# Layer 0's weight stream in the order of use, a key rotation on GpSimd, and folded squares

## The reference, cut to what matters

```python
def mla_mixer(h, cos, sin, w_a, g_q, w_uq, g_kv, w_ukv, w_o):
    a = h @ w_a                                   # 1024 -> 384 + 256 + 64
    cq, ckv, kr = jnp.split(a, [Q_LORA, Q_LORA + KV_LORA], axis=-1)
    q = (rms_norm(cq, g_q) @ w_uq).reshape(B, S, MLA_HEADS, NOPE_DIM + ROPE_DIM)
    q_nope = q[..., :NOPE_DIM]
    q_rope = apply_rope(q[..., NOPE_DIM:], cos[:, :, None], sin[:, :, None])
    kv = (rms_norm(ckv, g_kv) @ w_ukv).reshape(B, S, MLA_HEADS, NOPE_DIM + V_DIM)
    k_nope, v = kv[..., :NOPE_DIM], kv[..., NOPE_DIM:]
    k_rope = apply_rope(kr, cos, sin)
    ...                                           # masked softmax attention, o
    return o @ w_o

h = rms_norm(x, attn_pre_g[layer])                # x0; x1, x2, x3 are the next norms
```

## Time and profile before

| | us |
|---|---|
| median of 3 runs | 991.06 |
| lowest, highest | 990.77, 992.12 |
| the profiled execution | 990.73 |
| its span, first to last instruction | 988.6 |

### The profile page before, as it was taken

One profiled execution on the slowest core, in us unless ns is written; L12 is line 12 of the kernel. 1 busy time (PEld: TensorE's weight loads), 2 busy tenths in 40 slices (PEclk: granted clock), 3 DMA queues, 4 the chain that ended last, 5 costly groups with the idle time before them and its releaser, 6 DMA issues.

```text
span 988.6 us, 18855 instructions
## 1 busy us (share of the span) xinstructions
PE 959.7 (97%) x7951; PEld 923.9 (93%) x7951; DVE 721.8 (73%) x1342; ACT 542.7 (55%) x837; POOL 17.3 (2%) x48
## 2 busy tenths in 40 slices
PE   6999999999999999999999999999999999999997
PEld 6978999999998988799999998898999999999996
DVE  5965788887657877699878888646654879888653
ACT  6635565454436556565545444546755567676542
POOL 0000000000000000000000000000130000000000
PEclk9999999999999999999999999999999999999999
DMA  7433467676664742438666883543333545555521
GB/s 288 182 128 128 193 221 280 225 252 259 263 212 154 269 147 109 171 146 323 247 265 256 328 317 122 214 175 125 129 131 130 209 171 186 199 185 199 212 89 43
DMA packets 28452, 194.71 MB, mean 197 GB/s; under 512 B 3280, under 2 KB 3536, under 8 KB 5456
## 3 DMA queue, kind: packets, MB, share of 16 engines
q1 hardware_dynamic: 28368, 193.51, 52.7%
HBM read 192.45 MB, written 1.05 MB: 196 GB/s over the span
## 4 chain that ended last, share of the span: by engine, by line
PE 85%; DVE 7%; ACT 5%; issue 2%; DMA 1%; SPq 1%; POOL 0%; DVEq 0%; ACTq 0%
PE bank L495 24%; PE bank L496 23%; PE bank L501 23%; DVE s_wlo L1343 2%; PE bank L625 2%; PE bank L651 2%; ACT s_whi L883 2%; PE bank L556 2%; PE bank L550 2%; PE bank L551 1%; PE bank L515 1%; PE bank L522 1%; PE bank L516 1%; PE bank L635 1%; DMA s_raw<-in_wa 1%
## 5 line engine op out<-in xcount | busy, mean ns | idle before, releaser
L1343 DVE TENSOR_TENSOR s_wlo<-s_raw,s_whi 128x512 fp32r<-128x512 f32 (+1 forms) x364 | 371.3, 1061 | 141.1 <-ACT s_whi L883 140.7
L883 ACT ACTIVATE s_whi<-s_raw 128x1024 fp32r<-128x1024 f32 (+2 forms) x233 | 305.3, 1336 | 212.2 <-PE bank L501 198.2
L495 PE MATMUL bank<-s_hh,s_whi 128*128 128x256 f32 x1400 | 393.6, 281 | 0.4 <-DVE s_hl L1425 0.2
L496 PE MATMUL bank<-s_hl,s_whi 128*128 128x256 f32 x1400 | 387.6, 277 | 0.0
L501 PE MATMUL bank<-s_hh,s_wlo 128*128 128x256 f32 x1383 | 382.8, 277 | 0.0
L495 PEld LDWEIGHTS bank<-s_hh,s_whi 128*128 128x128 f32 x1400 | 263.3, 188 | 6.2 <-issue 5.1
L496 PEld LDWEIGHTS bank<-s_hl,s_whi 128*128 128x128 f32 x1400 | 263.1, 188 | 0.1
L501 PEld LDWEIGHTS bank<-s_hh,s_wlo 128*128 128x128 f32 x1383 | 259.8, 188 | 0.0
L495 PE MATMUL bank<-s_ph,s_whi 128*128 128x256 f32 x528 | 146.4, 277 | 0.0
L496 PE MATMUL bank<-s_pl,s_whi 128*128 128x256 f32 x528 | 145.8, 276 | 0.0
L501 PE MATMUL bank<-s_ph,s_wlo 128*128 128x256 f32 x516 | 142.5, 276 | 0.0
(11 more groups left out here) (237 smaller groups left out, 1278.9 us busy)
## 6 DMA issues: line engine op xcount, KB each, us to landing
s_raw<-in_gu SPq DMA_DIRECT2D x44, 1024.0 KB, 4.9
s_raw<-in_dn SPq DMA_DIRECT2D x33, 1024.0 KB, 4.8
s_raw<-in_wada SPq DMA_DIRECT2D x24, 1024.0 KB, 5.1
s_raw<-in_up SPq DMA_DIRECT2D x22, 1024.0 KB, 4.8
s_raw<-in_wo SPq DMA_DIRECT2D x8, 1024.0 KB, 4.8
s_raw<-in_win_g SPq DMA_DIRECT2D x8, 1024.0 KB, 4.8
s_raw<-in_wkv_v SPq DMA_DIRECT2D x4, 1024.0 KB, 5.3
s_raw<-in_wkv_k SPq DMA_DIRECT2D x4, 1024.0 KB, 4.8
```

The lines of the kernel that those rows point to most:

```text
L495: e.matmul(out, hi, xh[:, k, :], start=first, stop=False, skip_group_check=True)
L496: e.matmul(out, hi, xl[:, k, :], start=False, stop=False, skip_group_check=True)
L883: e.activation(whi[w % SPLIT][:, at], raw[p % RAW][:, at], ACT.Copy).then_inc(S.hi.tick((w, c0)), 1)
L1343: e.tensor_tensor(wlo[s][:, at], raw[p % RAW][:, at], whi[s][:, at].bitcast(F32), ALU.subtract).then_inc(S.lo.tick((i, j), (i, "all")), 1)
```

## The change

- **Loads.** The nine columns needed first (norm weight and frequencies), the positions and x become one tensor of 16 + 256 + 8 x 256 columns. SP loads it in two transfers, the first with the columns, the positions and two row blocks of x, the second with the other six. The first piece of `wa` comes in two halves, not in four quarters. The other columns (`cols`) are loaded after piece 2.
- **Programs at the start.** ACT and DVE have a new order for the splits of x and `wa`, the angles and the squares. ACT makes sine and cosine ahead of the squares and of its part of piece 1.
- **PE's first work.** PE starts with 16 matmuls of ones by ones, 128 columns, into a bank that nobody reads.
- **Layer 0's stream.** The tiles of `wuk`, `wuq` and `wuv` are laid in one weight stream `mla`, in the order in which PE uses them. Only `wuk` 0 to 3 stand ahead of `_order0()`; the other keys, the values and the queries are mixed with the softmax steps, with new paces and places.
- **Key rotation.** Its six operations move from DVE to POOL, behind POOL's constants.
- **Folds.** x0, x1, x2 and x3 get `fold` on DVE and one matmul of ones instead of two; the columns of x2 are two matmuls instead of four.

```diff
+WARM = 16
+FRONT = 16 + T
+MLA = ([("wuk", i) for i in range(4)] + [("wuq", i) for i in range(12)] +
+       [("wuk", i) for i in range(4, 8)] + [("wuq", i) for i in range(12, 24)] + [("wuv", i) for i in range(16)] +
+       [("wuk", i) for i in range(8, 12)] + [("wuq", i) for i in range(24, 30)] +
+       [("wuk", i) for i in range(12, 16)] + [("wuq", i) for i in range(30, 36)])
+MLA_AT = {unit: i for i, unit in enumerate(MLA)}
+STREAM = [("wa", 56), ("mla", 68), ("wo0", 64), ("gu0", 352), ("dn0", 176),
...
+PACE0 = {"wuk": 0.72, "wuq": 0.84, "wuv": 0.2, "wo0": 0.26}
+PAIR0 = (18, 18, 44, 44)
+AFTER0 = {**AFTER, "exp": ("scores", 9), "scale": ("exp", 3), "values": ("turn1", 7), "chunk": ("values", 0)}
+
+
 def _units(name):
     return [(name, t) for t in range(COUNT[name])]
 
 
 def _order0():
-    units = _units("wuq")[:16] + [("wuv", g) for g in range(8)] + _units("wuq")[16:] + _units("wo0")
-    return _mixed(units, _soft_steps(range(4)), {"wuq": 0.3, "wuv": 0.6, "wo0": 0.3},
-                  lambda p: ("wuq", (17, 29, 35)[p - 1]) if p else ("wuv", 0), "wo0", 2)
+    units = [(name, i // 2 if name == "wuv" else i) for name, i in MLA[4:] if name != "wuv" or i % 2 == 0] + _units("wo0")
+    return _mixed(units, _soft_steps(range(4)), PACE0, lambda p: units[PAIR0[p]], "wo0", 2, AFTER0)
...
-            e.dma_start(cols[:, 0:NFIRST], a["cols"][:, 0:NFIRST]).then_inc(S.gain_in.tick("gain"), 16)
-            e.dma_start(xT[:, 0:2, :], a["xT"][:, 0:2, :]).then_inc(S.x_in[0].tick("x"), 16)
+            first = FRONT + 2 * T
+            e.dma_start(x_front[:, 0:first], a["xT"][:, 0:first]).then_inc(S.x_in[0].tick("x"), 16)
...
                 if i == 0:
-                    for c in range(4):
-                        into = S.first_in[c] if c < 3 else S.raw_in[0]
-                        e.dma_start(dst[:, 512 * c:512 * (c + 1)], src[:, 512 * c:512 * (c + 1)]).then_inc(
-                            into.tick(0), 16)
-                        if c == 0:
-                            e.dma_start(posi, a["pos"]).then_inc(S.pos_in.tick("pos"), 16)
-                        if c in (1, 3):
-                            at = slice(c + 1, c + 3)
-                            e.dma_start(xT[:, at, :], a["xT"][:, at, :]).then_inc(S.x_in[(c + 1) // 2].tick("x"), 16)
-                    e.dma_start(xT[:, 6:8, :], a["xT"][:, 6:8, :]).then_inc(S.x_in[3].tick("x"), 16)
-                    e.dma_start(cols[:, NFIRST:NCOL], a["cols"][:, NFIRST:NCOL]).then_inc(S.cols_in.tick("cols"), 16)
+                    e.dma_start(dst[:, 0:1024], src[:, 0:1024]).then_inc(S.first_in.tick(0), 16)
+                    e.dma_start(x_front[:, first:], a["xT"][:, first:]).then_inc(S.x_in[1].tick("x"), 16)
+                    e.dma_start(dst[:, 1024:2048], src[:, 1024:2048]).then_inc(S.raw_in[0].tick(0), 16)
                 else:
                     e.dma_start(dst[:, 0:k * P], src).then_inc(S.raw_in[i % RAW].tick(i), 16)
+                if i == 2:
+                    e.dma_start(cols[:, NFIRST:NCOL], a["cols"][:, NFIRST:NCOL]).then_inc(S.cols_in.tick("cols"), 16)
...
-                        e.matmul(out[:, T + b:T + b + 1], sq[:, b * P:(b + 1) * P], ones[:, 0:1], start=True, stop=False)
-                        m = e.matmul(out[:, T + b:T + b + 1], sq[:, T + b * P:T + (b + 1) * P], ones[:, 0:1],
-                                     start=False, stop=True)
+                        for half in range(acc):
+                            at = half * T + b * P
+                            m = e.matmul(out[:, T + b:T + b + 1], sq[:, at:at + P], ones[:, 0:1], start=half == 0,
+                                         stop=half == acc - 1)
...
+            q.wait_ge(S.const, "ones")
+            for _ in range(WARM):
+                e.matmul(banks[7][:, 0:P], ones[:, :], ones[:, :], start=True, stop=True, skip_group_check=True)
             q.wait_ge(S.const, "ready")
             lead("wa", 4, 8, hh, hl, "h0", (0, 1), S.dve_out)
-            sums("x0", 7)
+            sums("x0", 7, acc=1)
             tiles("wa", 4, 1, 8, hh, hl, "h0", 2, S.dve_out)
             tiles("wa", 5, 2, 8, hh, hl, "h0", 3, S.dve_out)
             tiles("wuk", 0, 2, 2, cqh, cql, "cq", 4, S.dve_out)
             sums("kv", 6, columns=True)
...
-            tiles("wuk", 2, 2, 2, cqh, cql, "cq", 5, S.dve_out)
-            sums("q", 7)
-            for n in (4, 6):
-                tiles("wuk", n, 2, 2, cqh, cql, "cq", (0, 1)[n // 2 - 2], S.dve_out)
...
+            x_high(0)
+            x_high(1)
+            hi_part(2)
+            hi_part(2)
+            for k in range(2, 6):
+                x_high(k)
+            hi_part(2)
+            hi_part(2)
+            x_high(6)
+            x_high(7)
             q.wait_ge(S.rot, "angle")
             q.wait_ge(S.const, "ready")
             e.activation(sinb, tmp[2][:, :], ACT.Sin).then_inc(S.trig.tick("sin"), 1)
             e.activation(tmp[0][:, :], tmp[2][:, :], ACT.Abs).then_inc(S.trig.tick("abs"), 1)
             q.wait_ge(S.trig, "abs")
             e.activation(cosb, tmp[0][:, :], ACT.Sin, scale=-1.0, bias=epsc[:, 1:2]).then_inc(S.trig.tick("cos"), 1)
+            x0_square(0)
+            hi_part(2)
+            hi_part(2)
+            x0_square(1)
+            x0_square(2)
+            hi_part(3)
+            x0_square(3)
+            hi_part(3)
...
+            angle(0)
+            angle(1)
+            x_low(0)
+            angle(2)
+            x_low(1)
+            lo_part(1)
+            angle(3)
+            lo_part(1)
+            for k in range(2, 6):
+                x_low(k)
+                angle(k + 2)
+            lo_all(1)
+            x_low(6)
+            x_low(7)
+            lo_all(2)
             for i in (1, 2, 3):
                 square_sum("x0", i, sqv[i])
+            fold("x0")
...
-            q.wait_ge(S.dve_out, ("cq", 6))
-            rotate(tmp[3][:, :], tmp[4][:, :], A0.K[:, 8, :], A0.K[:, 9, :], "k")
             lo_all(_used_up("wa", 48) + SPLIT)
-            for n in (0, 2, 4, 6):
-                scaled_out("wuk", n, 2, Rs[1], "kv", lambda m: A0.K[:, m, :])
-                if n == 2:
-                    lo_all(_used_up("wa", 56) + SPLIT)
+            lo_all(_used_up("wa", 56) + SPLIT)
+            scaled_out("wuk", 0, 2, Rs[1], "kv", lambda m: A0.K[:, m, :])
 
...
@@ vector_program, in its walk over _order0()
+                elif step == "wuk":
+                    if i % 4 == 3:
+                        scaled_out("wuk", i // 4 * 2, 2, Rs[1], "kv", lambda m: A0.K[:, m, :])
+                    if i % 2 == 1:
+                        lo_part(_mla_used(step, i) + SPLIT)
...
@@ vector_program, behind the squares of x1; the same line for x2 and x3
+            fold("x1")
...
+            q.wait_ge(S.trig, "cos")
+            q.wait_ge(S.dve_out, ("cq", 6))
+            e.tensor_tensor(tmp[0][:, :], tmp[4][:, :], sinb, ALU.mult)
+            e.tensor_tensor(tmp[1][:, :], tmp[3][:, :], sinb, ALU.mult)
+            e.tensor_tensor(A0.K[:, 8, :], tmp[3][:, :], cosb, ALU.mult)
+            e.tensor_tensor(A0.K[:, 9, :], tmp[4][:, :], cosb, ALU.mult).then_inc(S.rot_k.tick("products"), 1)
+            q.wait_ge(S.rot_k, "products")
+            e.tensor_tensor(A0.K[:, 8, :], A0.K[:, 8, :], tmp[0][:, :], ALU.subtract)
+            e.tensor_tensor(A0.K[:, 9, :], A0.K[:, 9, :], tmp[1][:, :], ALU.add).then_inc(S.rot_k.tick("k"), 1)
```

More of the change, by code:

```diff
@@ L45 @@
           ("up2", 704 // 2), ("dn2", 176)]
-FINE = ("wa", "wuk", "wuv", "wuq", "wo0", "dn0", "wkv_v", "wkv_k", "wq1", "wo1", "dn1", "win_v", "win_k", "win_q", "win_g")
+FINE = ("wa", "mla", "wo0", "dn0", "wkv_v", "wkv_k", "wq1", "wo1", "dn1", "win_v", "win_k", "win_q", "win_g")
 def _stream():
@@ L138, in _stick_steps, with _mixed @@
             yield "keep", p
-def _mixed(units, steps, paces, pair_at, chunk_name, per=1):
+def _mixed(units, steps, paces, pair_at, chunk_name, per=1, after=AFTER):
     steps, ahead, at, made, credit = iter(steps), [], {}, set(), 0.0
@@ L159, in ready @@
         else:
-            need, tiles = (AFTER[name][0], i), AFTER[name][1]
+            need, tiles = (after[name][0], i), after[name][1]
         return need in at and n >= at[need] + tiles
@@ L374, in col @@
             at = COLS[name][0] + j
-            return cols[:, at:at + n]
+            return x_front[:, at:at + n] if at < NFIRST else cols[:, at:at + n]
         def tile_out(name, j):
@@ L684, in tensor_program @@
             for step, i in _order0():
-                if step == "wuq":
+                if step == "wuk":
+                    n, k = i // 2, i % 2
+                    if n % 2 == 0 and k == 0:
+                        bank_of["wuk", n] = (4, 0, 1, 3)[n // 2]
+                        take(bank_of["wuk", n], S.dve_out, ("wuk", n))
+                    q.wait_ge(S.xlo, ("cq", k))
+                    product("wuk", i, banks[bank_of["wuk", n - n % 2]][:, (n % 2) * T:(n % 2 + 1) * T], cqh, cql, k,
```

(33 more changed lines are left out.)

72 lines of the change are left out of this document (38 added, 34 removed).

## The result

| | before | after |
|---|---|---|
| median, us | 991.23 (4 runs) | 983.32 (4 runs: 982.33 to 984.05) |
| profiled execution, its span | 990.73, 988.6 | 982.33, 980.3 |

The ratio is 0.9923, 95% interval 0.9909 to 0.9937: 7.9 us or 0.8% faster. The forecast was 984.6 us, 6.5 us gained, in a range from 981.5 to 988.5. The two profiled executions differ by 8.4 us, and nearly all of that arises in the first 110 us of the program.

What follows compares the result with a forecast made beforehand. PE was taken as the bound, busy in 97% of the span, with DVE full beside it in layer 0. Gains of 2.6, 3.0 and 0.9 us made 6.5 off 990.73, or 984.2; the median forecast was 984.6, range 981.5 to 988.5.

Steps and rivals of the forecast that it cites:

- two signs of being wrong: PE waiting for `s_wlo` between 20 and 43 us, or the first rows of x landing later than 4.7 us.
- Loads and the first product: Start of layer 0: x at 8.2, piece 1 at 12, k = 2 at 12.6; x0's sum ends at 22.3 instead of 24.9.
- The clock behind the wait for k = 2: PE's standstill of some 2 us there may lower its clock, costing 1.7 us; half of it was taken.
- PE at the first scores: PE, with 5.6 us less work ahead of layer 0's first scores, arrives there at 43.4.
- DVE at the first scores: DVE starts `cq` at 23.7 and is ready at 43.7, which sets the first scores: 2.6 us gained.
- POOL's price: Key rotation in layer 0: six POOL operations cost DVE 0.35 us each, 2.1 in all, from possible 0 to 10.5.
- rival in which POOL holds DVE off: Key rotation: operations of 1.2 us, nine tenths lost, cost DVE 6.5 us; ready at 48.1, total 989.0. Chance 0.09.
- Behind the first scores: Layer 0 after the first scores: 3.6 us of PE waits go, less 0.6 for new ones: 3.0 us gained.
- deduction of 0.6 for new waits: Behind the first scores, new short waits because DVE has more keys and a rotation there: 0.6 us lost.
- Folds: Folds outside layer 0's start: x1 gains 0.43, x2 0.43 and 0.40, x3 loses 0.35; 0.9 us gained.
- all in time: No clock fall, POOL free beside DVE: x0's sum at 21.0, PE at 42.1, total 982.3. Chance 0.13.
- the new order is worth only its filled place at the output unit: Waits behind the first scores stay; only the filled place at `wo0` pays, 1.4 instead of 3.0: 986.2. Chance 0.08.

Runs made afterwards that it cites:

- e6: The changed kernel without the sixteen matmuls of ones on PE: 982.37 us, ratio 0.9911.
- e1: The kernel before with the new start alone (loads, new order of ACT and DVE, matmuls of ones, fold of x0): 989.02 us, ratio 0.998.
- e5: The changed kernel with the key's rotation back on DVE: 982.08 us, ratio 0.9906.
- e7: The changed kernel with DVE's four parts of the value weights behind the first evictions and the queries' rotation, and x3 unfolded: 981.28 us, ratio 0.9896.
- e9: The changed kernel once more, unaltered, as the yardstick for e10: 982.66 us, ratio 0.9908.
- e10: The changed kernel with the key's rotation back on DVE, measured beside e9: 981.59 us, ratio 0.99.
- e2: The kernel before with layer 0's new stream and order alone, rotation still on DVE and the old start: 986.08 us, ratio 0.9952.
- e4: The kernel before with the folds of x1, x2 and x3 alone: 990.23 us, ratio 0.999.
- e3: The kernel before with the key's rotation on POOL alone: 989.64 us, ratio 0.9987.
- e11: The kernel of e8 with the key's rotation back on DVE: 979.80 us, ratio 0.9881.
- e12: The kernel of e8 once more, unaltered: 979.63 us, ratio 0.9883.
- e8: e7 plus, at the start, one low part of piece 0 between x's splits and ACT's first high part of piece 1 before the sine: 979.68 us, ratio 0.9882.

## Why the prediction was right

Sign, size and most steps hold; 983.32 lies 1.3 us below the forecast, and neither of its two signs of being wrong came (the first x is used at 4.00, and PE waits for no `s_wlo` between 20 and 43 us). Between the two profiled executions 8.4 us were gained where the sum said 6.5.

- **Loads and the first product: right in place.** x was forecast for 8.2, seen at 8.61; k = 2 for 12.6, seen at 12.86; piece 1 was no longer waited for. A late k = 0 (7.79) cost nothing, and the ones were worth nothing, as costed and as e6 shows. The two lists of SP's issues differ by six, not by five as the prediction has it; no number of its sum hangs on that.
- **The clock behind the wait for k = 2: it falls in some executions.** Half of 1.7 us was put in. In the profiled execution the clock stayed up, so x0's sum ends at 21.7 (21.29 and two rows of 0.22), not at 22.3. In e1, e5 and e7, with a start of the same loads and a wait of 1.9 to 2.0 us, it fell, and the sum stood at 22.94, 22.91 and 22.54; in e9 and e10 it did not. That is three of six, at 1.5 to 1.7 us each. An average was the right thing to put in; no execution shows it.
- **PE at the first scores: forecast 1.3 us too late.** It was to arrive at 43.4 and came at 42.1 (the row at 43.60 less its wait and a part explained below): 0.6 from x0's sum, 0.7 because the stretch took 20.4 us instead of 21.1. The 0.118 us per matmul, which the forecast took as fixed, was not: behind x0's sum 256 columns took 0.116 us on average, from start to start, where before they took 0.120. As DVE was last here, this gained nothing.
- **DVE at the first scores: right, 43.7 against 43.60.** It began at 23.61 (forecast 23.7). POOL's price was put at 2.1 us; it was 1.64 in longer parts and 0.47 in a new wait for ACT, together 2.1. The agreement of the total is partly luck, since the wait for ACT was not foreseen and both numbers vary (e9: 2.13 and 0.67). The rival in which POOL holds DVE off had the right mechanism with too high a price: most operations met DVE for 1.2 us but cost it only about 0.4. The Trainium skill, "SBUF — State Buffer", section "Who interferes with whom", says that a DVE instruction with two SBUF inputs contends with a GpSimd instruction that reads SBUF, and that the port pair which the two share is an exclusive lock; here the trace agrees, and it shows the loss on either side, POOL's (2.84 for 0.74) or DVE's (4.13 for 2.49). The Trainium skill's "GPSIMD Engine Reference", section 3.1, has POOL's add at 1.96 times DVE's time; free rows here are 0.74 us against 0.42, 1.8 times.
- **Behind the first scores: the term that was mis-sized, 4.9 us instead of 3.0.** Idle time of PE behind the first scores fell from 1.29 + 0.46 + 1.79 + 0.42 = 3.96 us to 0.42, 3.5 gained, as the gross 3.6 said. The deduction of 0.6 for new waits was for nothing: there are none. And each wait cost more than its idle time. The profile counts idle from a matmul's end, but a matmul of 256 columns takes 0.28 us and the next starts 0.12 after the start of the first, so that a wait costs its idle time and 0.16 us more. Behind three transposes it costs 0.26 more: from 73.98 to 76.27 are 2.29 us, and the same step without a wait takes 0.24. From start to start the four waits before cost 1.44, 0.62, 2.05 and 0.68, together 4.8 us, and the one that is left 0.58: 4.2 of the 4.9 us. The other 0.7 is spread over short gaps and was not separated. e2 shows that all 4.9 belong to the order alone.
- **Folds: 0.7 us against 0.9,** in e4 and behind the sum of 101.73 alike. x3's fold loses, as said: the wait behind the sum is 0.67 us (forecast 0.9).
- **The parts add up.** e1 to e4 gave 1.9, 4.9, 1.3 and 0.7, together 8.8 us, against 7.9 and 8.6 for the whole, which was measured twice. Each part is uncertain by about 1 us or more, so this is agreement and no proof. The start gave 1.9 where its expectation said 3.4; in its profile the clock fell behind k = 2, so that 2.7 us arrived at the first scores, and again behind the output unit, where 1.6 of them went. How much of that the median holds isn't shown. In the changed kernel the wait at the output unit is gone, and more of the gain can stay.

Of the rivals, "all in time" (982.3) describes the profiled execution's PE side (no fall of the clock, 3.6 us of waits gone) but not POOL. That the new order is worth only its filled place at the output unit is refuted by e2.

What stays open: by what way the rotation on POOL costs the changed kernel about 1 us, as the times of e5 and e10 have it, when the stretches of the profiles differ by nothing. The granted clocks of the single executions point to the clock: their mean is 0.997 over the nine with POOL's rotation (the result and e9) and 0.998 over the eight with DVE's (e5 and e10), and a difference of 0.001 would be 1 us of 981 if all of it counted. A price could come in by way of the wait at the scores, 1.34, 1.83 and 1.35 us with the rotation on POOL, if it lets the clock fall in some executions, but the rotation on DVE has waits of 0.90 and 1.55 there as well. In e11 and e12, where PE doesn't wait there, the two places cost the same. It also stays open why a wait is followed by a fall in one execution and not in the next.

## What to carry to other kernels

Read what a wait costs from start to start, not from its idle time alone, and count a wait as long as the ones of 1.8 us here as a risk on top: removing it also removes executions in which the clock falls behind it. Before moving work off a full engine, look at the operand traffic of the engine that gets it and at the next engine that the first would catch up with; here two small costs (1.64 and 0.47 us) ate a saving of 2.3, and the times were 1 us longer all the same. An earlier start is worth only what the engine that is last at the next meeting point gives, so the reordering of DVE's parts in e7 and e8 paid 3.0 to 3.6 us (with x3 unfolded) on top of a start that alone had brought 1.9.
